# Output weights loaded into the place of x's low parts while attention ends, and ten low parts of the first merge block on GpSimd

## The reference

```python
merged = (gates[:, :, 0] * einsum('bsc,cd->bsd', y_a, w_up_a)
          + gates[:, :, 1] * einsum('bsc,cd->bsd', y_b, w_up_b)
          + gates[:, :, 2] * einsum('bsc,cd->bsd', y_c, w_up_c))
out = einsum('bsd,de->bse', merged, w_out)
x = layer_norm(ALPHA * x + out, ln_g, ln_b)
```

## Time and profile before

| | us |
|---|---|
| median of 3 executions | 1962.34 (1961.93 to 1962.75) |
| profiled execution, its own time | 1960.81 |
| span of its trace, first to last instruction | 1959.3 |
| PE busy | 1914.8 (98% of the span) |
| DVE busy | 1123.9 (57%) |
| ACT busy | 707.9 (36%) |
| POOL busy | 434.9 (22%) |

### The profile page before, as it was taken

One profiled execution on the slowest core, in us unless ns is written; L12 is line 12 of the kernel. 1 busy time (PEld: TensorE's weight loads), 2 busy tenths in 40 slices (PEclk: granted clock), 3 DMA queues, 4 the chain that ended last, 5 costly groups with the idle time before them and its releaser, 6 DMA issues. The chain is left out here.

```text
span 1959.3 us, 30551 instructions
## 1 busy us (share of the span) xinstructions
PE 1914.8 (98%) x10560; PEld 1625.1 (83%) x10560; DVE 1123.9 (57%) x2142; ACT 707.9 (36%) x1090; POOL 434.9 (22%) x548
## 2 busy tenths in 40 slices
PE   8999999999999999999999999999999989999998
PEld 6878887888887888888888788888888878999997
DVE  4564226654244655646465665565655568777776
ACT  3111013121034555555555655555555532111110
POOL 2927930498000000000000000000000002222322
PEclk9999999999999999999999999999999999999999
DMA  7223225322422141231523515133142276555642
GB/s 191 70 84 116 86 86 199 63 104 107 146 102 93 50 138 55 76 114 47 138 61 87 180 50 139 59 84 108 48 135 65 84 254 215 167 175 170 173 118 87
DMA packets 104569, 221.69 MB, mean 113 GB/s; under 512 B 11001, under 2 KB 56745, under 8 KB 100905
## 3 DMA queue, kind: packets, MB, share of 16 engines
q1 hardware_dynamic: 90736, 161.41, 26.3%
q0 software_dynamic: 12608, 55.19, 10.2%
q10 hardware_dynamic: 1152, 4.19, 0.5%
HBM read 155.09 MB, written 65.08 MB: 112 GB/s over the span
## 5 line engine op out<-in xcount | busy, mean ns | idle before, releaser
L1439 PE MATMUL g_ps<-x_hi,w_lo 128*128 128x512 f32 x768 | 310.1, 404 | 0.0
L1439 PE MATMUL g_ps<-x_hi,w_hi 128*128 128x512 f32 x768 | 309.2, 403 | 0.0
L1355 DVE TENSOR_TENSOR pt_lo<-t_ps,pt_hi 128x512 fp32r<-128x512 f32 (+2 forms) x320 | 190.6, 607 | 140.8 <-ACT pt_hi L1261 140.4
L1439 PE MATMUL g_ps<-x_lo,w_hi 128*128 128x512 f32 x768 | 226.6, 410 | 4.0 <-PEq L1476 2.6
L695 PE MATMUL tile_ps<-x_hi,w_hi 128*128 128x512 f32 x736 | 228.4, 391 | 0.0
L695 PE MATMUL tile_ps<-x_hi,w_lo 128*128 128x512 f32 x736 | 226.7, 389 | 0.0
L695 PE MATMUL tile_ps<-x_lo,w_hi 128*128 128x512 f32 x736 | 226.6, 389 | 0.0
L1261 ACT ACTIVATE pt_hi<-t_ps 128x512 fp32r<-128x512 f32 (+2 forms) x320 | 170.3, 533 | 143.4 <-PE t_ps L1398 138.6
L1293 DVE CUSTOM_DVE_ANT_0 s_sb<-s_ps,f_row 128x512 f32<-128x512 f32 (+2 forms) x320 | 181.8, 604 | 35.0 <-PE s_ps L1387 34.2
L1169 POOL DMA_DIRECT2D mixT<-y_out x63 | 33.8, 536 | 749.5 <-DVE y_out L1307 749.5
L1398 PE MATMUL t_ps<-ident,s_sb 128*128 128x128 f32 x1088 | 172.1, 273 | 9.5 <-DVE pt_lo L1355 5.1
(11 more groups left out here) (288 smaller groups left out, 3569.8 us busy)
## 6 DMA issues: line engine op xcount, KB each, us to landing
w_lo_raw<-in_w_tiles SPq DMA_DIRECT2D x96, 512.0 KB, 3.6
gateT<-g_out SPq DMA_DIRECT2D x96, 256.0 KB, 3.0
gate<-gateT SPq DMA_DIRECT2D x64, 384.0 KB, 4.5
qkvT<-zout SPq DMA_DIRECT2D x24, 512.0 KB, 3.2
x_lo_raw<-in_xT SPq DMA_DIRECT2D x20, 512.0 KB, 8.6
silT<-zout SPq DMA_DIRECT2D x16, 512.0 KB, 2.7
k_ll<-qkvT POOLq DMA_DIRECT2D x16, 512.0 KB, 6.5
q_st<-qkvT POOLq DMA_DIRECT2D x16, 512.0 KB, 8.7
```

What stands on the lines that cost most here:

```text
L1355: dve.tensor_tensor(pt_lo[part], t_ps[n % 2][:, 0:keys].rearrange("p (k q) -> p k q", q=P), pt_hi[part].bitcast(F32), ALU.subtract).then_i ...
L1439: mm = pe.matmul(g_ps[c][:], w[j % 2][:, k, :], x[:, k, c * BANK:(c + 1) * BANK], start=(r == 0), stop=(r == 3 * KT - 1))
```

## The change

The raw tensor of w_out gets a fixed place at x_lo's address, kept over the stages. SP issues its eight loads (512 KB each: two k, one half of the columns) at the end of the last phase of attention, four for each c as soon as the last matmul that reads that half of x_lo has run. ACT's eight issues in the merge go. ACT splits wo_hi 0 ahead of block 0 and one wo_hi per tile from tile 1 on. On DVE, the low part of w_up moves behind the second sum and is done in tiles 0 to 2 only (w_up tiles 3, 4, 5); the low parts of w_up tiles 6 and 7 and all eight of w_out are done by POOL, ahead of its loads of x, ln_g and ln_b. PE waits for those on a semaphore of POOL's, low_split.

```diff
+        self.wo_raw = nc.alloc_sbuf_tensor_at("wo_raw", [P, KT, D], F32, offset=nc.sbuf_base + 4 * KT * HALF)
+        self.wo_loaded = [sem(f"wo_loaded{i}") for i in range(KT // 2)]
...
+                        if phase == 1 and u == 1:
+
+                            sp.wait_ge(x_lo_used, 2 * NCH * T_GATE - NCH + c + 1)
+                            cols = slice(c * BANK, (c + 1) * BANK)
+                            for k in range(0, KT, 2):
+                                sp.dma_start(kept.wo_raw[:, k:k + 2, cols], io["w_out"][:, k:k + 2, cols]
+                                             ).then_inc(kept.wo_loaded[k // 2], 16)
                         store((T_GATE - 2 + u) * P, now, (m0 + T_GATE - 2 + u) * 2 + c, c)
...
+        wo_lo, wo_raw, wo_loaded = sb("wo_lo", [P, KT, D], F32R), kept.wo_raw, kept.wo_loaded
...
-        wo_lo, wo_raw = low_with_raw(nc, ctx, "wo_lo", [P, KT, D])
...
                     act.activation(m_hi[:, d], gate[d % RING][:, 0], ACT.Copy, scale=0.5).then_inc(m_high, 1)
-                    if first and d < KT // 2:
-                        for k in range(2 * d, 2 * d + 2):
-                            act.dma_start(wo_raw[:, k, :], io["w_out"][:, k, :]).then_inc(wo_loaded[k // 2], 16)
                     if first and d + EARLY + 1 < KT:
                         split_wu(d + EARLY + 1)
-                    if first and d >= KT // 2:
-                        for k in range(2 * d - KT, 2 * d - KT + 2):
-                            split_wo(k)
+                    if first and d:
+                        split_wo(d)
                 if not last:
                     high_y(b + 1)
                 root(b, 0)
 
             for i in range(EARLY_SPLIT, EARLY + 1):
                 split_wu(i)
+            split_wo(0)
...
-                    if first and d + EARLY < KT:
-                        low_wu(d + EARLY)
-                    elif first:
-                        low_wo(d + EARLY - KT)
...
                     dve.tensor_tensor(g[:, 0], g[:, 0], g[:, 2], ALU.add).then_inc(merged, 1)
+                    if first and d + EARLY < KT - 2:
+                        low_wu(d + EARLY)
                 split_m(b, KT - 1)
-                if first:
-                    for k in range(EARLY, KT):
-                        low_wo(k)
...
-                    if first:
+                    if first and d < KT - 2:
                         pe.wait_ge(wu_split, d + 1)
+                    elif first:
+                        pe.wait_ge(low_split, d - KT + 3)
                     if not first or d >= 2:
...
-                                pe.wait_ge(wo_split, k + 1)
+                                pe.wait_ge(low_split, k + 3)
...
-            pool.wait_ge(lifted, KT)
+            for i in range(KT - 2, KT):
+                pool.wait_ge(wu_high, i + 1)
+                pool.tensor_tensor(wu_lo[i][:], wu_raw[i], wu_hi[:, KT - 1 - i].bitcast(F32),
+                                   ALU.subtract).then_inc(low_split, 1)
+            for k in range(KT):
+                pool.wait_ge(wo_high, k + 1)
+                pool.tensor_tensor(wo_lo[:, k], wo_raw[:, k], wo_hi[:, k].bitcast(F32), ALU.subtract).then_inc(low_split, 1)
             for c in range(NCH):
                 pool.wait_ge(kept.g_stored[c], 16 * (2 * T_GATE + 1))
             pool.wait_ge(kept.last_y_stored, 16)
```

More of the change, by code:

```diff
@@ L1538, in stage_merge @@
         wu_loaded = [sem(f"wu_loaded{i}") for i in range(EARLY, KT)]
-        wo_loaded = [sem(f"wo_loaded{i}") for i in range(KT // 2)]
         gate_loaded = [kept.gate0_loaded, *(sem(f"gate_loaded{i}") for i in range(1, RING))]
@@ L1544, in stage_merge @@
         out_stored = [sem(f"out_stored{m}") for m in range(2)]
-        (ln_loaded, wo_high, wo_split, lifted, weighted, part_sum, merged,
+        (ln_loaded, wo_high, low_split, lifted, weighted, part_sum, merged,
          m_high, m_split, h_full, h_sum, h_stats, h_mean, h_var, h_root, h_rstd, h_norm, h_scaled, h_out, h_part, tail, last_stored) = (
             sem(n) for n in (
-                "ln_loaded", "wo_high", "wo_split", "lifted",
+                "ln_loaded", "wo_high", "low_split", "lifted",
                 "weighted", "part_sum", "merged", "m_high", "m_split", "h_full", "h_sum", "h_stats", "h_mean",
@@ L1657, in low @@
                 dve.tensor_tensor(dst, src, hi.bitcast(F32), ALU.subtract).then_inc(done, 1)
-            def low_wo(k):
-                dve.wait_ge(wo_high, k + 1)
-                low(wo_lo[:, k], wo_raw[:, k], wo_hi[:, k], wo_split)
             def low_wu(i):
```

## The result

The changed kernel takes 1972.33 us (median; 1971.29 to 1974.85, 5 runs) against 1961.93 (1959.12 to 1962.75, 5 runs) of the kernel before on the same chip: ratio 1.0052, 95% interval 1.0041 to 1.0063, so **10.4 us slower**. The forecast said 1967.8, +5.5: the sign and the range held, the size was too small by nearly half.

A forecast was written before the change was run, and what follows sets the result against it. TensorE was taken as the bound, with 12.3 us of block 0 above its unstalled 44.60 us. Profiled 1960.81 + 1.5 (block 0) + 4.0 (block 1) = 1966.3; from the median, 1962.34 + 5.5 = 1967.8, range 1960 to 1974.

The forecast's parts named there:

- Part 1: End of attention: w_out loads on SP cost nothing; late gates' 11.76 us gone; wu 3 lands near 1588.
- Part 2: Block 0's up projection: new DVE and ACT order, ending at 1608.4 against 1613.6, 5.2 us gained.
- Part 3: Block 0: POOL's ten low parts hold DVE's two-SBUF-input operations and give the 5.2 us back; net +1.5 us.
- rival B: Block 0: POOL's low parts do not hold DVE; 3.5 to 4.3 us faster, 1958.0 to 1958.8; chance 0.20.
- by the row it is not: Argument against a falling PE clock: in 1616 to 1620 PE was busy 2.19 of 4 us at clock 1.00.
- Rival D: Block 0's output product: PE's clock falls while PE is paced by POOL, half idle; 1971; chance 0.10.
- step 7 doubles: Block 0's output product: price of a fallen PE clock on step 7, 1.4 us.
- A: Main case: POOL's low parts hold DVE in block 0, block 1's data comes late; 1964 to 1972; chance 0.55.
- Part 4: Start of block 1: mix lands late, about 1639, and PE waits 2.1 us; +4 us (0 to 6).

The follow-up runs named there:

- before_mix_early: The kernel before with block 1's mix loads issued behind the fourth low part of block 0, nothing else changed: 1962.17 us, ratio 0.9999.
- dve_all_lows: The changed kernel with all thirteen low parts of block 0 on DVE, early load and new order kept: 1959.33 us, ratio 0.998.
- mix_early_dve_lows: dve_all_lows with block 1's mix loads issued behind the fourth low part of block 0 instead of the eighth: 1956.59 us, ratio 0.9968.
- pool_blank_lows: The changed kernel with GpSimd's ten subtracts replaced by memsets over the same columns, which read nothing: 1958.99 us, ratio 0.9981.
- x_load_first: The changed kernel with GpSimd's four loads of x and ln moved ahead of its eight wo_lo: 1973.15 us, ratio 1.0053.
- mix_early_pool_lows: The changed kernel with block 1's mix loads issued behind the fourth low part of block 0 instead of the eighth: 1968.22 us, ratio 1.003.
- half_load_late: dve_all_lows with the second half of the output weights' columns loaded by SyncE in the merge: 1960.31 us, ratio 0.9991.

## Why the prediction was right in sign and too small

- **Part 1, early load.** Right that it costs nothing at the end of attention: the four issues ahead of the last stores took 2.40 us from 1577.01, and the store behind them left at 1581.47. Right that the gates would be in time. Mis-sized: up tile 3 was put near 1588 and landed at 1591.1, which is 1589.8 when the stage's later start of 1.3 us is taken off: 8.02 us in the chain, where before_mix_early has 5.66. At the third merged sum 0.8 us of this lateness was left.
- **Part 2, order.** u was to end 5.2 us sooner than before with two tiles held; it ended 3.45 sooner (28.25 us after the first matmul, for 31.70). Tile 7 began at 1608.57, behind the gate product of tile 5, which stood behind a held sum, and not at the end of wu_lo 7 (1607.27), as forecast. Without GpSimd's part the gain is there: u ends 4.6 us sooner in dve_all_lows and 5.35 in mix_early_dve_lows, and block 0 is shorter by 4.8 and 5.5. The order alone gave no gain (+1.0 in the trace), and the early load beside GpSimd's subtracts none; the early load in the old order, with all low parts on VectorE, wasn't run.
- **Part 3, the lock.** The mechanism was right in its rows: 2.4 to 2.5 us a subtract, sums at 2.6, the gate product free, the last subtract waiting for ACT. It is shown by pool_blank_lows, and rival B falls with it. That VectorE gets an operation through behind each subtract held in the changed kernel, but not in x_load_first. Block 0 was to be 1.5 us longer than before and was 4.7 longer. The first of two terms: the last subtract ended 47.4 us after the first u matmul instead of 46.1. Of these 1.35 us 0.45 was there at the end of wu_lo 7, behind up tile 3. The other 0.9 came in the row of wo_lo, where the seventh subtract waited 1.76 us for ACT as the eighth did, while the forecast let seven run in a row. The second term is the clock.
- **The step that failed: "by the row it is not".** Rival D had been judged by a window in which PE, busy 2.19 of 4 us, kept its clock; but the wait in that window was of 1.28 us (before 1617.84). In the changed kernel the steps with 0.9 us of wait kept the clock too; behind the gaps of 2.52 and 1.71 us ahead of the last two steps it fell. The same working had put a gap of 2.8 there (step 6 from 1623.8 to 1625.2, the last subtract's end at 1628.0), and it wasn't held against the row. From 1630.82 nine steps at 1.36 would have ended at 1643.1, and ended at 1644.7: 1.7 us, the term "step 7 doubles" nearly alone. The rule cited beside D (the Trainium skill, TensorE: Matmul & The Clock Gate, section on psum-queue depth-cycling), on clocks that go up and down with short idle times between groups, the trace bears out for gaps of about 2.5 us, not for those of 0.9. So the 1972.3 is A with most of D, and lies nearest D's 1971, which had a chance of 0.10.
- **Part 4, block 1.** +5.0 for +4, the near hit in part luck. Right: the mix came late and PE waited for it, 3.08 us for the 2.1 of the working. The mix landed at 1643.4, which is 1642.1 with the 1.3 us taken off, and not 1639; SP needed 4.7 us to issue the eight loads (1628.19 to 1632.93), and they shared full DMA engines (1.02 busy) with x and ln. The up to 2.5 us more that GpSimd's two layer-norm operations were to cost didn't come: a sum was held (2.48 us), but PE waited nowhere behind 1653.78. In their place 1.8 us went into a clock of 0.83 and 0.75 behind the wait (18.93 us for 144 matmuls that take 17.1), which the forecast did not hold at all. mix_early_pool_lows shows that the mix is the whole of it.

Summed: 3.2 us short in block 0, 1.0 in block 1, and 0.7 that the medians show above the trace. TensorE's clock after a wait took 1.7 us in block 0 and 1.8 in block 1.

What stays open: ten subtracts gave a block 0 of 61.5, 63.4, 63.7 and 63.8 us in four kernels. Late gates stand in the chain of the second, a later up tile 3 explains most of the third, the issues on GpSimd and the long hold the fourth. What lets VectorE through between two subtracts in three of them and not in x_load_first wasn't tried.

## What to carry to other kernels

Before work is moved to GpSimd to relieve VectorE, look whether VectorE's remaining operations have two SBUF inputs and whether GpSimd's would read SBUF: then a GpSimd instruction can stop a VectorE instruction for its whole length (0.42 us became 2.6), a row of five stopped one for 12.99 us, and a chain that passes through both engines is paid twice. Try each part of a change alone: here the early load and the order were together worth 4 us, hidden behind a part that cost 14. When a forecast puts a wait of 2 us or more into TensorE's path, price the clock behind it as well.

## What was not expected of the hardware

- TensorE's clock fell behind gaps of 2.5 us in the changed kernel, and held at 1.00 through steps with 0.9 us of wait in each. It isn't the gap alone: in mix_early_pool_lows a gap of 2.52 us passed at 1.00, and the clock fell only after the next, of 2.97:

```profile
1624.00:1628.00 4.00, 1.48 (x7) 0.91 (x7) 3.97 (x4) 1.28 (x2) 2.38 (x1) 1.00 0.39 89
1628.00:1632.00 4.00, 1.50 (x6) 0.90 (x6) 3.42 (x5) 2.60 (x4) 2.50 (x1) 1.00 0.62 131
1632.00:1636.00 4.00, 3.53 (x11) 2.81 (x12) 3.90 (x7) 1.90 (x3) 2.45 (x5) 0.70 0.69 241
```

- GpSimd writing three memsets over 2304 columns in 2.3 us held nothing on VectorE.
- A hold need not end with the GpSimd instruction: in x_load_first one sum stood still over five subtracts in a row, which then ran at 2.35 us each instead of 2.53.
- Up tile 3, a load of 512 KB, landed 7.7 to 9.5 us after its issue in the seven runs with all 4 MB of output weights issued ahead of it (6 and 13 us ahead in the changed kernel, where they themselves took 9.7 us, median). With half of them ahead it took 4.3 (half_load_late). "Early enough" for one transfer made the next one late.
